# SiLU of the gates z moved into the projection stage, and squares of q and k taken by GpSimd, in a hybrid attention and gated DeltaNet layer

## The reference, cut to what matters

```
c = silu(causal_conv(x_ext, conv_w))                 # q, k, v of the delta branch
qb, kb, vb = split(c)
qb = qb * rsqrt(sum(qb * qb) + eps)                  # per head of 128; kb likewise
ob, s_new = gated_delta_rule(qb, kb, vb, g, beta, s0)   # chunks of 64 tokens
ob = rms_norm(ob, delta_norm_w) * silu(z)            # 4 heads x 128
y_b = ob @ w_proj_b
```

## Time and profile before

| | us |
|---|---|
| median of 3 runs | 2150.34 |
| lowest and highest of them | 2143.91, 2155.2 |
| profiled execution | 2142.44 |
| its span in the profile | 2140.7 |
| projection with its slabs, about | 65 to 614 |
| attention, about | 614 to 855 |
| delta stage, about | 855 to 1113 |
| tail, about | 1113 to 2141 |

### The profile page before, as it was taken

How to read it: one execution, slowest core, us unless ns; L and a number is a source line. 1 busy time by engine, 2 the same in 40 slices (tenths; PEclk the granted TensorE clock), 3 DMA queues, 4 the chain that set the end, 5 groups by cost and what they waited for, 6 DMA issues and landing times. The chain is left out here.

```text
span 2140.7 us, 34184 instructions
## 1 busy us (share of the span) xinstructions
PE 1980.2 (93%) x13954; PEld 1780.6 (83%) x13954; DVE 801.0 (37%) x1579; ACT 656.4 (31%) x1241; POOL 584.8 (27%) x455
## 2 busy tenths in 40 slices
PE   4999999999987777788869999999999999999998
PEld 3899999999984455677759987988889999999996
DVE  3111577111136886354545319122222222222225
ACT  5100222100024554344444325422222222222222
POOL 8021121112100000423325414422223333333233
PEclk7999999999997998799969999999999999999999
DMA  4122222622234220231014324211111111111114
GB/s 121 53 94 93 72 94 89 231 83 94 83 136 159 82 77 1 81 100 42 27 60 150 114 92 145 63 40 40 40 40 40 42 56 41 40 47 43 40 55 162
DMA packets 159272, 169.18 MB, mean 79 GB/s; under 512 B 14188, under 2 KB 130044, under 8 KB 159151
## 3 DMA queue, kind: packets, MB, share of 16 engines
q1 hardware_dynamic: 152814, 141.52, 21.7%
q10 hardware_dynamic: 6336, 25.96, 3.0%
HBM read 126.84 MB, written 40.55 MB: 78 GB/s over the span
## 5 line engine op out<-in xcount | busy, mean ns | idle before, releaser
L2252 DVE TENSOR_TENSOR t_acc<-t_acc,t_B 128x512 f32<-128x512 f32 x252 | 173.1, 687 | 541.0 <-PE t_B L2345 541.0
L116 PE MATMUL i_ps<-x_hi,i_w_lo 128*128 128x384 f32 x1056 | 354.0, 335 | 0.0
L116 PE MATMUL i_ps<-x_lo,i_w_hi 128*128 128x384 f32 x1056 | 353.8, 335 | 0.0
L116 PE MATMUL i_ps<-x_hi,i_w_hi 128*128 128x384 f32 x1056 | 353.8, 335 | 0.0
L2332 PE MATMUL t_B<-t_merged_hi,t_wm_lo 128*128 128x384 f32 x768 | 256.9, 335 | 1.0 <-POOL t_wm_lo L1957 1.0
L2332 PE MATMUL t_B<-t_merged_lo,t_wm_hi 128*128 128x384 f32 x768 | 256.6, 334 | 0.0
L2332 PE MATMUL t_B<-t_merged_hi,t_wm_hi 128*128 128x384 f32 x768 | 256.6, 334 | 0.0
L106 POOL TENSOR_TENSOR i_w_lo<-i_w_raw,i_w_hi 128x1024 fp32r<-128x1024 f32 x44 | 104.9, 2385 | 444.6 <-ACT i_w_hi L101 444.6
L1957 POOL TENSOR_TENSOR t_wm_lo<-t_raw,t_wm_hi 128x1024 fp32r<-128x1024 f32 x49 | 118.6, 2421 | 296.1 <-ACT t_wm_hi L2032 296.1
L116 PEld LDWEIGHTS i_ps<-x_hi,i_w_lo 128*128 128x128 f32 x1056 | 199.2, 189 | 0.0
L116 PEld LDWEIGHTS i_ps<-x_lo,i_w_hi 128*128 128x128 f32 x1056 | 199.1, 189 | 0.0
(11 more groups left out here) (318 smaller groups left out, 3497.8 us busy)
## 6 DMA issues: line engine op xcount, KB each, us to landing
proj<-i_out ACTq DMA_DIRECT2D x44, 576.0 KB, 2.8
i_w_raw<-in_w_in SPq DMA_DIRECT2D x44, 512.0 KB, 3.9
t_raw<-in_w_up SPq DMA_DIRECT2D x32, 512.0 KB, 4.3
t_raw<-in_w_down SPq DMA_DIRECT2D x32, 512.0 KB, 3.6
t_gates<-proj SPq DMA_DIRECT2D x48, 192.0 KB, 2.6
a_k_cache<-in_cache_attn_k SPq DMA_DIRECT2D x8, 1024.0 KB, 5.6
a_v_cache<-in_cache_attn_v SPq DMA_DIRECT2D x8, 1024.0 KB, 5.3
d_c<-proj SPq DMA_DIRECT2D x3, 1536.0 KB, 7.1
```

The source lines that it names most:

```text
L116: last = pe.matmul(out, a[s][:, c, :], b[:, c, tokens], start=k == 0, stop=k == n - 1)
L2252: dve.tensor_tensor(a, a, B[(ND * j + d) % 4][:, :], ALU.add).then_inc(added, 1)
```

## The change

It has two parts.

In the projection stage the four slabs of z get a loop of their own, in ACT's queue and in DVE's: DVE copies the banks to `y` instead of `st`, and ACT puts the SiLU from `y` into `st` and stores that. In the delta stage the SiLU of z is gone, and DVE waits for the landing of z in "turn" (L1561 after) where ACT waited in "mean".

"sums" moves from ACT to POOL for the groups 1 to 4; in group 0 ACT keeps it. There are two buffers `sq`, one for q and one for k, and the semaphore `sq_read` is gone; the second buffer lies on memory that earlier stages used for `level` and `state_t`.

```
@@ stage_in_proj, scalar
-            plain(NZ // 2, HALF - 1)
+            with act.Fori(NZ // 2, NZ // 2 + 2) as i:
+                for s in range(2):
+                    split_hi(act, w, i + 1, s)
+                    evacuated(i, s)
+                    act.wait_ge(sent[s], 16 * i + 16)
+                    act.activation(st[s][:, :], y[s][:, :], ACT.Silu).then_inc(silued, 1)
+                    act.wait_ge(silued, 2 * i + s - NA + 3)
+                    store(act, i, s)
+            plain(NZ // 2 + 2, HALF - 1)
@@ stage_in_proj, vector
-            plain(NZ // 2, HALF)
+            with dve.Fori(NZ // 2, NZ // 2 + 2) as i:
+                for s in range(2):
+                    dve.wait_ge(silued, 2 * i + s - NA + 1)
+                    for g in range(NTG):
+                        dve.wait_ge(prod, 3 * (2 * i + s) + g + 1 + CREDIT)
+                        dve.tensor_copy(y[s][:, g * TG:(g + 1) * TG], ps[3 * s + g][:, 0:TG]).then_inc(free, 1)
+            plain(NZ // 2 + 2, HALF)
@@ stage_delta
-        sq = at("sq", [P, HB, 4 * L], top + 2 * 4096)
+        sq = [at(f"sq{i}", [P, HB, 4 * L], a) for i, a in enumerate((top + 2 * 4096, env.level_at))]
@@ stage_delta, gpsimd
+                if kind == "grp" and s == "sums":
+                    w = L * len(GROUPS[n])
+                    pool.wait_ge(c_in[n % 2], 16 * ((n + 1) // 2))
+                    wait(pool, "pe", "grp", n - 1, "sums")
+                    for i in range(2):
+                        half_c = C[n % 2][:, 4 * i:4 * i + 4, 0:w]
+                        pool.tensor_tensor(sq[i][:, :, 0:w], half_c, half_c, ALU.mult).then_inc(sq_made, 1)
+                    continue
@@ stage_delta, scalar
                     elif s == "sums":
+                        act.wait_ge(env.c_in, 32)
                         for i in range(2):
...
-                            if i:
-                                act.wait_ge(sq_read, n + 1)
-                            elif n:
-                                wait(act, "pe", "grp", n - 1, "sums")
-                            ins = act.activation(sq[:, :, 0:w], C[n % 2][:, 4 * i:4 * i + 4, 0:w], ACT.Square)
-                            ins.then_inc(sq_made, 1)
+                            act.activation(sq[i][:, :, 0:w], C[0][:, 4 * i:4 * i + 4, 0:w], ACT.Square).then_inc(sq_made, 1)
...
-                    act.activation(rso[:, tiles, :], rso[:, tiles, :], ACT.Sqrt)
-                    act.wait_ge(z_in, 16 * sum(len(GROUPS[i]) // 2 for i in range(n + 1)))
-                    ins = act.activation(z[:, :, 0:w], z[:, :, 0:w], ACT.Silu)
+                    ins = act.activation(rso[:, tiles, :], rso[:, tiles, :], ACT.Sqrt)
@@ stage_delta, vector, "turn" of the finals
+                        dve.wait_ge(z_in, 16 * sum(len(GROUPS[i]) // 2 for i in range(n + 1)))
```

More of the change, by code:

```diff
@@ L1048, in has @@
         if kind == "grp":
-            return {"decay": ("pool", "pe", "act"), "sums": ("act", "pe", "dve"), "cols": ("pe", "act", "dve")}[s].count(eng)
+            return {"decay": ("pool", "pe", "act"), "sums": ("pool" if n else "act", "pe", "dve"), "cols": ("pe", "act", "dve")}[s].count(eng)
         if kind == "prep":
@@ L1064, in stage_delta @@
             for i, item in enumerate(x for x in SCHED if x[0] == kind and has(eng, x)
-                                     and not (eng == "act" and x[2] in ("sums", "out"))):
+                                     and not (eng in ("act", "pool") and x[2] in ("sums", "out"))):
                 place[(eng, *item)] = i + 1
@@ L1091, in stage_delta @@
     c_in = sems(env, "d", "c_landed0", "c_landed1")
-    z_in, sq_made, sq_read, gates, gsum, gexp, cleared, dstep, osq, own, sent, mem4_made = sems(
-        env, "d", "z_landed", "sq_made", "sq_read", "gates", "gate_sums", "gate_exps", "cleared", "dstep", "o_squared",
+    z_in, sq_made, gates, gsum, gexp, cleared, dstep, osq, own, sent, mem4_made = sems(
+        env, "d", "z_landed", "sq_made", "gates", "gate_sums", "gate_exps", "cleared", "dstep", "o_squared",
         "state_sent", "states_sent", "member4")
@@ L1584, in _ @@
                             for h in range(HB):
-                                last = pe.matmul(Z7[32 * h:32 * h + 32, 0:w], env.pick[:, 31 - i:63 - i], sq[:, h, 0:w],
+                                last = pe.matmul(Z7[32 * h:32 * h + 32, 0:w], env.pick[:, 31 - i:63 - i], sq[i][:, h, 0:w],
                                                  start=i == 0, stop=i == 1)
-                            if i == 0:
-                                last.then_inc(sq_read, 1)
                     else:
@@ L2422, in build @@
             env.cum, env.after = (sb(n, [P, 2, P], c=mix) for n in ("cum", "after"))
+            env.level_at = (nc.sbuf_base + 31) // 32 * 32
             env.level = sb("level", [P, len(LEVELS), P], c=mix)
+            env.state_t = sb("state_t", [P, CC, NB * (CW - 1)], c=mix)
+            assert nc.sbuf_base - env.level_at >= 4096
             env.member = sb("member", [P, 2 + NB], c=mix)
@@ L2433, in build @@
             env.c0 = nc.alloc_sbuf_tensor_at("d_c0", [P, CC, 256], F32, offset=env.c_at)
-            env.state_t = sb("state_t", [P, CC, NB * (CW - 1)], c=mix)
             env.conv_tail = sb("conv_tail", [P, CC, (NB + 1) * (CW - 1)], c=mix)
```

## The result

| | kernel before | changed | difference |
|---|---|---|---|
| median, first comparison | 2147.12 us (4 runs, 2143.42 to 2155.2) | 2113.23 us (4 runs, 2110.81 to 2116.4) | -33.9 |
| median, on another chip | 2144.95 us (11 runs) | 2115.33 us (4 runs) | -29.6 |
| profiled execution, first pair | 2142.44 us | 2116.4 us | -26.0 |
| span | 2140.7 us | 2114.6 us | -26.1 |

The ratio is 0.9845, with a 95% interval of 0.9817 to 0.9873, and on the other chip 0.9854, 0.9827 to 0.9881. The forecast was 19 us faster, 2131, with a range from 2120 to 2143. The prediction was wrong in size.

A forecast was written before the change was run, and what follows sets the result against it. The delta stage was taken as latency-bound, PE waiting on chains through ACT or DVE. Waits of -14.7 us and 4 of clock gave -19, so 2131 us from the 2150.34 median, range 2120 to 2143.

The forecast's parts named there:

- Waits ahead of 4b: Delta stage, groups 1 to 4: without table load and SiLU, copies for 4b start 2.25 us earlier each, 9.0 gained.
- Loads ahead of "cols": Delta stage, groups 2 to 4: table loads before "cols" go, gaining 0.8, 0.8 and 1.28, together 2.9 us.
- End of the stage: After the delta stage's last "mean": two table loads and a SiLU go, "norm" starts 2.9 us earlier.
- Second buffer: In "sums", PE no longer waits for the second square: 3.3 us gained in groups 2 to 4, 1.2 in group 0.
- Group 1's loss: POOL's squares in group 1 stand behind four state scalings, so PE's second set of products starts 4.6 us later.
- Rival 5: Projection: the new z loop delays each of four slabs by 4 us; -3 us net, 2147, chance 0.03.
- The sum of the waits: All gains and the loss in the delta stage on an unchanged clock: -14.7 us.
- the clock: PE's low-clock time in the delta stage shrinks with shorter idle times: 0 to about 11 us, 4 taken.
- The base: Whole kernel: the 19 us gain was set on the runs' median, 2150.34 us, not the profiled 2142.44, giving 2131.
- Rival 1: Delta stage: the clock falls in the same places as before; -14.7 us, 2136, chance 0.22.
- Rival 3: Delta stage, group 1: the larger gap leaves PE at low clock until 4b; +2 us, 2153, chance 0.05.
- Rival 2: Delta stage: POOL and DVE hinder each other, a square costs 2.35 us; 2136 to 2138, chance 0.09.

The follow-up runs named there:

- e14: Changed kernel plus idle TensorE products in the idle places it has left; 2117.32 us, 27.4 below the kernel before, ratio 0.9875.
- e13: Kernel before plus idle TensorE products in all idle places of groups 1 to 4, the stage's end and the tail's start; 2131.88 us, ratio 0.9942.
- e9: Kernel before plus idle TensorE products, cut to fit, ahead of 4b and between the squares of groups 1 to 4; 2132.17 us, ratio 0.9932.
- e8: Kernel before, unchanged, in a second profiled execution; 2152.99 us.
- e12: Kernel before, unchanged, in a third profiled execution; 2148.84 us.
- e5: Kernel before plus oversized idle TensorE products ahead of 4b and zero products between squares, groups 1 to 4; 2151.87 us, ratio 1.0029.

## Why the prediction was wrong in size

- **Waits ahead of 4b, right.** Forecast 4 x 2.25; from the square root to the copies the profiles have 2.47 less 0.12, so 2.35, four times.
- **Loads ahead of "cols", right, a little low.** 0.8, 0.8 and 1.28 forecast; 1.03, 1.02 and 1.43 found from ACT's last copy of a group to the first of the next. I had capped each gain at PE's idle time before "turn", and 0.2 us more came through.
- **End of the stage, right.** 2.9 forecast, 3.0 found in both pairs, unfilled and filled, from DVE's last "mean" to "norm". "norm" follows the root after 0.27 us of idle time:

```profile
1083.22 0.18 DVE L1556 RECIPROCAL d_vec<-d_vec 128x4 f32<-128x4 f32 x1 [0.27 <-ACT d_vec L1412]
```

- **Second buffer, right.** The 1.24, 1.24 and 0.81 us are gone. Group 0 gained 1.5 where 1.2 was forecast.
- **Group 1's loss, right.** Forecast 4.6 later for PE's second set. Counted from the last step before it that both kernels share (ACT's squares of the streams' outputs, at 901.56 before and 897.01 after) it is 4.4 later.
- **SiLU in the projection at no cost, right.** Rival 5 is out.
- **The sum of the waits, right.** 14.7 forecast. PE's idle time fell by 14.4, e14 and e13 lie 14.6 apart, and the places above add up to 16.3 (9.4 + 3.5 + 3.0 + 3.3 + 1.5 - 4.4).
- **The failed step: the clock.** I wrote "at most ... about 11 us. At least: nothing ... I take 4, nearer to the low end". The waits give 14 to 16 of the 29.6 to 33.9 us, so the clock gave 13 to 19: three to five times what I took, and more than my bound. Two things were off. The bound came from the low stretches of one execution, which with 67 us at the low level had the least of three; for the pair of profiles with that execution it holds, since there PE's busy time fell by 11.6 us and the stage itself, without the 2 us ahead of it, leaves about 10 beside the waits. But even that is more than twice the 4 I took. I had reasoned from how many gaps would remain, although the trace had it: apart from the start of the stage and the gap of group 1, each low stretch before (945, 990, 1045 and 1085 us) follows one of the gaps that the change closes or shortens. e9 shows that closing just two kinds of gap keeps the clock up.
- **The base.** I set the gain from a profile with 2142 us on a median of 2150, as if the 8 us between them were measurement and would stay. By e8 and e12, 10.6 and 6.4 us above that profile at equal waits, such a difference is low clock, and the change takes a part of it as well. The first thing to distrust was the scatter of the runs itself, 11 us.
- **Rival 1** (clock unchanged, 14.7) has the right number for the waits and fell with the clock. **Rival 3** (slower, by a low clock behind the larger gap in group 1) did not happen: with 7.7 us of idle time the clock fell to 0.50, and was back at 1.00 from 910 on. **Rival 2** (POOL and DVE in each other's way) is seen, at a small size. Where "norm" starts behind POOL's second square it takes longer, 1.50 us for 1.22, and a small product 0.46 for 0.16:

```profile
982.99 3.75 POOL L1251 TENSOR_TENSOR d_sq<-d_c 128x1024 f32<-128x1024 f32 x2 [8.25 <-DMA d_c<-proj]
986.32 1.50 DVE L1557 TENSOR_TENSOR d_o<-d_o,d_vec 128x1024 f32<-128x1024 f32 x1
...
1025.30 0.46 DVE L1552 SCALAR_TENSOR_TENSOR d_vec<-d_vec 128x8 f32<-128x8 f32 x1
```

Each is 0.3 us, and the squares themselves took 1.87 and not 2.35. "norm" met the last 0.4 us of POOL's square and lost 0.3 of them; with the rule that the prediction takes from the Trainium skill ("SBUF — State Buffer", the shared port pair) this agrees as far as it goes, and an overlap by a whole square was not seen here.

What stays open: why the clock stays low for longer in one execution than in another, and how the clock's gain divides among the single gaps. The attention stage, which no variant touches, ended from 856 to 862 us by the delta stage's first instruction on ACT, by kernel and by run; that is another part of the scatter, up to 6 us, and its cause was not looked for.

## What to carry to other kernels

A wait that TensorE sits through in a latency-bound stage can cost its length and then the low clock behind it; here the second was about as large as the first (14 to 16 and 13 to 19 us). Size the clock's term from several executions, by time at the low level, and not from one profile; if the executions of one kernel scatter by 11 us at equal waits, that scatter is part of what a change of the gaps can win. To find out how much of a gain is clock, fill the gaps of both kernels with idle products that fit them and compare those; the fillers' own cost stays in the answer.

## What the hardware showed that was not expected

- An idle product cost twice what I took from the transposes. 16 products of 64 output rows into the same half of a bank took 3.71 us in e9 (row x32, two records a product), 32 with 128 rows 7.41 in e5, so 0.232 each either way; PE's "turn" makes 32 in 3.71, alternating between two halves. By these times products into different halves ran beside each other here, and four quarters did better still: 10 zero products with 32 rows took 0.82 us (row x20), 0.082 each.

```profile
946.71 0.82 PE L1589 MATMUL d_B<-ident,pick 128*32 128x128 f32 x20
```

- A busy PE stayed at the low level for longer in one execution of a kernel than in another: in e8 for two windows in a row, 5.00 of 5.00 us busy at 0.50, twice over. Which execution draws the long stretch I could not tell.
